# A high part stored 64 bytes further on in a one-core block kernel (convolution, attention, linear attention, mixture of experts)

## The reference, cut to what matters

```python
merged = merged + jax.nn.sigmoid(h @ w_merge_gate[l, n]) * (y_b @ w_branch[l, n])
...
x = x + merged @ w_out[l]
h2 = rms_norm(x, norm_ffn[l])
x = x + hier_moe(h2, ...)
```

## Time and profile before

| What | us |
|---|---|
| median of 3 runs (706.58 to 706.75) | 706.69 |
| the profiled execution's own time | 708.88 |
| its span, first to last instruction | 707.1 |
| PE busy | 584.7 |
| PE weight loads busy (beside PE) | 409.9 |
| DVE busy | 301.2 |
| ACT busy | 191.1 |
| GpSimd busy | 29.7 |

### The profile page before, as it was taken

One profiled execution on the slowest core, in us unless ns is written; L12 is line 12 of the kernel. 1 busy time (PEld: TensorE's weight loads), 2 busy tenths in 40 slices (PEclk: granted clock), 3 DMA queues, 4 the chain that ended last, 5 costly groups with the idle time before them and its releaser, 6 DMA issues.

```text
span 707.1 us, 15475 instructions
## 1 busy us (share of the span) xinstructions
PE 584.7 (83%) x6644; PEld 409.9 (58%) x6644; DVE 301.2 (43%) x627; ACT 191.1 (27%) x335; POOL 29.7 (4%) x58
## 2 busy tenths in 40 slices
PE   7999999999999999996777678666687657778575
PEld 5887899999999885553343334333343324334342
DVE  6476976975475955442222322223222232222312
ACT  5584454564444443111110101001011100111011
POOL 2612000000000020000000000000000000000000
PEclk9999999999999999998787878878779896878987
DMA  9995446446579799999999999999999999999993
GB/s 312 310 362 185 130 145 218 146 149 210 197 273 418 305 388 342 416 426 426 426 428 427 427 425 426 426 425 429 425 426 426 426 428 428 424 426 427 424 415 142
DMA packets 39716, 247.78 MB, mean 350 GB/s; under 512 B 4408, under 2 KB 6592, under 8 KB 25568
## 3 DMA queue, kind: packets, MB, share of 16 engines
q1 hardware_dynamic: 37184, 245.44, 86.0%
q0 software_dynamic: 912, 1.25, 1.0%
q10 hardware_dynamic: 1552, 0.10, 0.2%
HBM read 245.72 MB, written 1.06 MB: 349 GB/s over the span
## 4 chain that ended last, share of the span: by engine, by line
PE 55%; DMA 39%; another core or an unknown queue 2%; DVE 1%; issue 1%; ACT 0%; SPq 0%; DVEq 0%; ACTq 0%
DMA wide<-in_w_expert_up 34%; PE ps L1414 10%; PE ps L1050 7%; PE ps L1052 7%; PE ps L1051 7%; DMA wide<-in_w_expert_down 5%; PE ps L1449 4%; PE ps L1374 3%; PE ps L1023 3%; PE ps L1025 3%; PE ps L1024 3%; PE ps L1461 2%; PE ps L1429 1%; PE ps L1383 1%; DMA x_tok<-in_x 1%
## 5 line engine op out<-in xcount | busy, mean ns | idle before, releaser
L1414 PE MATMUL ps<-wide,xe 128*32 128x256 f32 x2048 | 163.3, 473 | 109.4 <-DMA wide<-in_w_expert_up 108.7
L1414 PEld LDWEIGHTS ps<-wide,xe 128*32 128x32 f32 x2048 | 76.7, 131 | 176.1 <-issue 133.4
L1943 DVE TENSOR_TENSOR xe<-ps,g_ffn 128x256 f32<-128x256 f32 x32 | 13.6, 425 | 256.8 <-PE ps L1383 256.7
L1538 DVE TENSOR_TENSOR ring_lo<-ring,w_hi 128x1024 fp32r<-128x1024 f32 x76 | 91.4, 1222 | 40.2 <-ACT w_hi L745 39.9
L745 ACT ACTIVATE w_hi<-ring 128x1024 fp32r<-128x1024 f32 x76 | 78.9, 1057 | 55.1 <-PE ps L1052 34.9
L1050 PE MATMUL ps<-hT_hi,w_hi 128*128 128x256 f32 x320 | 89.3, 279 | 0.6 <-DVE hT_lo L1554 0.6
L1051 PE MATMUL ps<-hT_lo,w_hi 128*128 128x256 f32 x320 | 88.4, 276 | 0.0
L1052 PE MATMUL ps<-hT_hi,ring_lo 128*128 128x256 f32 x320 | 88.4, 276 | 0.0
L946 ACT ACTIVATE he<-ps 128x128 f32<-128x128 f32 x32 | 8.9, 278 | 207.0 <-PE ps L1429 204.4
L1449 PE MATMUL ps<-wide,he 128*32 128x256 f32 x1024 | 62.5, 382 | 0.9 <-DMA wide<-in_w_expert_down 0.8
L1050 PEld LDWEIGHTS ps<-hT_hi,w_hi 128*128 128x128 f32 x320 | 60.1, 188 | 1.1 <-DVE ring_lo L1538 0.8
(11 more groups left out here) (284 smaller groups left out, 773.7 us busy)
## 6 DMA issues: line engine op xcount, KB each, us to landing
wide<-in_w_expert_gate SPq DMA_DIRECT2D x27, 2048.0 KB, 45.5
wide<-in_w_expert_up SPq DMA_DIRECT2D x27, 2048.0 KB, 48.6
wide<-in_w_expert_down SPq DMA_DIRECT2D x27, 2048.0 KB, 41.1
ring<-in_w_in SPq DMA_DIRECT2D x8, 2048.0 KB, 14.7
ring<-in_w_merge_gate SPq DMA_DIRECT2D x6, 2048.0 KB, 9.8
wide<-in_w_expert_gate SPq DMA_DIRECT2D x10, 1024.0 KB, 13.4
wide<-in_w_expert_up SPq DMA_DIRECT2D x10, 1024.0 KB, 9.3
wide<-in_w_expert_down SPq DMA_DIRECT2D x9, 1024.0 KB, 9.4
```

Source lines behind the costliest of these rows:

```text
L1414: ins = t_.matmul(ps[q * WIN:(q + 1) * WIN, b, 0:QW], xe[b][:, k % 2, k // 2, :], w, start=(k == 0), stop=(k == KD - 1))
L1538: v.tensor_tensor(piece(ring_lo, g, c), piece(ring, g, c), by_row(out_hi[g == 19][c]).bitcast(F32), ALU.subtract).then_inc(wpre_lo, 1)
```

## The change

`out_hi` begins 64 bytes later, now 128 above a multiple of 256 and still from `gv`'s place on. So that its end does not meet `scr`, `scr` and everything that shares its bytes begin 128 bytes later, now 192 above a multiple of 256. No other tile moves, and no instruction, wait, DMA or order of work is added, removed or exchanged.

```diff
@@ -230,13 +230,14 @@
         att_at = here_at[0]
         attm = here("attm", [P, 8, P], F32)
         gv_at = here_at[0]
-        out_hi = [w_hi, [place(f"out_hi{c}", [P, CW], F32R, at=gv_at + 4 * CW * c) for c in range(CHUNKS)]]
+        out_hi = [w_hi, [place(f"out_hi{c}", [P, CW], F32R, at=gv_at + 64 + 4 * CW * c) for c in range(CHUNKS)]]
         gv = here("gv", [P, TT, C], F32)
         gr_at = here_at[0]
         gr = here("gr", [P, TT, C], F32)
         kdn = here("kdn", [P, TT, 256], F32)
         sbd_at = here_at[0]
         sbd = here("sbd", [P, 3, 2, 256], F32)
+        here_at[0] += 2 * 64
         scr_at = here_at[0]
         scr = here("scr", [P, 2, C], F32)
```

## The result

The change makes the kernel slower: 710.19 us median (709.84 to 712.1, five runs) against 706.69 (706.55 to 706.75, five runs). The ratio is 1.0044, with an interval of 1.0026 to 1.0061. The forecast was 706.7 and no difference; the range ended at 707.6.

The account below looks back on a forecast made before the run. PE was taken to bound the kernel until about 275 us, then the expert weights' stream at some 426 GB/s. All terms were zero, so 706.69 + 0 = 706.7 us; the range was 705.9 to 707.6.

Parts of the forecast that it names:

- ACT, DVE and PE on `out_hi`: Operations writing, reading or streaming `out_hi` around the output projection: zero change; PE between 0.45 us less and 0.20 more.
- The row of `ring_lo`: Eight matmuls streaming `ring_lo` at 128 past `merged_hi`: 0.1175 us each, taken as showing that `out_hi` gains nothing at 128.
- `scr` and its sharers: Tiles in `scr`'s bytes, moved to 192: zero, up to 0.46 us more, of which `yc_hi` at the slow pace 0.30.
- The name says only half: Rival at 156 to 168 us: `yc_hi`, not the output projection, moves the time; 0.30 us more, 707.0 us; chance 0.05.
- Two reads of PE meet: Rival on `out_hi` matmuls: load and stream at the same offset modulo 128 delay each other; 0.45 us less, 706.2; chance 0.12.
- The pick of rows: Rival at line 1374, first three experts: picks streaming `xn2_0` each grow 0.5 us; 1.5 us more, 708.2 us; chance 0.05.
- The small terms: GpSimd's `xn2_0` write, `w_z` matmuls, DVE's branch sums and the final store: each taken as zero, with small bounds.
- the estimate: First final store, `fin0`: 134 beats in place of 130 per row, 3% more, landing 0.1 us later.
- Delays of PE reach the end: Before the router's end: a delay of the output projection shifts the DMA gaps and the end, at most one for one.
- The chances: For the kernel's time: 0.87 no difference, 0.06 faster and 0.07 slower by over 0.2%.

Follow-up runs that it names:

- experiment 7: Changed kernel, `yc_hi` back at 64, both `merged` parts at 192: 711.25 us, ratio 1.0046; smaller move, `merged_lo` left at 128, `scr` and `yc_hi` at 64: 708.31 us, 0.9997.

## Why the prediction was wrong

**ACT, DVE and PE on `out_hi`: right.** The tile view of the changed kernel:

```profile
L1264 PE MATMUL ps<-out_hi,merged_hi x32: 274/281/363, 246.5 to 261.8; 128*128 128x256 f32 x32
...
L885 ACT ACTIVATE out_hi<-ring x4: 1042/1042/1044, 239.8 to 242.7; 128x1024 fp32r<-128x1024 f32 x4
L1539 DVE TENSOR_TENSOR ring_lo<-ring,out_hi x4: 1216/1216/1218, 241.1 to 244.5; 128x1024 fp32r<-128x1024 f32 x4
```

ACT went from 1043 to 1042 ns, DVE from 1222 to 1216, the matmuls kept their median of 281. Their pace in the second pass is that of the earlier trace rows, 15 steps in 1.77 us:

```profile
250.68 0.28 PE L1264 MATMUL ps<-out_hi,merged_hi 128*128 128x256 f32 x1
...
252.45 0.28 PE L1267 MATMUL ps<-out_hi,merged_lo 128*128 128x256 f32 x1
```

The chain has this pass and the picks behind it at the same 2.7 us of delay, and with `out_hi` moved alone the kernel is unchanged. The row of `ring_lo` that I chose for this term was the right one for the matmuls that load `merged_hi`. For the other half, which load `merged_lo` at 128, it says nothing: I overlooked that their distance goes from 192 to 0. That they cost nothing is partly luck. Before the change they alternate with matmuls at 0 and 64 and ran at 0.118 already, and experiment 7 shows that the quarters get faster only where all that follow one another lie at 192.

**`scr` and its sharers: the term of the sum that failed is `yc_hi`, taken as zero.** I wrote that "the tiles at 64 and at 128 differ by less than a nanosecond" and that the slow pace would cost at most 64 x 0.0047 = 0.30 us. Both steps fail. The rows that I compared, in the quarters, lie at 64 and at 0 and 192 by turns, and both stretches are slow; that they agree says nothing about a series that lies at 192, the one fast distance, as a whole and is made to leave it. The row that could have said it was in my own hands: the branch's 113.3 against the quarters' 118, which I took as the scale of the effect but not as a sign that the place of `yc_hi` decides. And the bound counted only the matmuls that stream the moved tile. The measured price is 2.99 us, ten times the 0.30, because PE keeps the slow pace through the 608 other matmuls of the unbroken series. The pace per matmul, 0.0047, was right to 0.3 ns.

**The rivals.** *The name says only half* was right about the place (from 156 us, `yc_hi`, not the output projection) and wrong in size, 707.0 for 710. *Two reads of PE meet* had the right kind of mechanism, the relation of streamed and loaded tile, with the wrong rule: not the same offset modulo 128 but one of six distances modulo 256 is the good one, and the new place of `out_hi` does not reach it. *The pick of rows* did not get slower: 1.00 us, as before.

**The small terms: right.** GpSimd's write of `xn2_0`, the matmuls on `w_z`, DVE's sums and the store of the result in the changed kernel, by timeline and tile views:

```profile
258.84 4.03 POOL L705 TENSOR_SCALAR xn<-x_tok,stat 128x1024 f32<-128x1024 f32 x1 [141.66 <-DVE stat L1851]
```

```profile
L1079 PE MATMUL ps<-hT_hi,w_z x16: 379/379/403, 22.7 to 23.8; 128*32 128x256 f32 x16
```

```profile
L1794 DVE TENSOR_TENSOR xn_merged<-xn_merged,scr x8: 691/692/693, 196.3 to 237.6; 128x512 f32<-128x512 f32 x8
```

```profile
DMA to landing us min/median/max: 2.7/3.0/3.4
```

4.03 us against 3.98, 379 ns against 379, 692 ns against 692, and landings of 2.7 to 3.4 us in both the earlier trace rows. The 3% that the Trainium skill's page "DMA: Bandwidth & Descriptors" would add to the first store's beats do not show: that store is the shorter of the two, and in the records it lands 2.69 us after its issue in both kernels, where the estimate asked for 0.1 us more. The measurement decides against the estimate here.

**Delays of PE reach the end: right.** A delay of 2.7 us ahead of the router became 0.44% at the end (3.1 us by the ratio), "at most one for one" within its interval of 1.8 to 4.3 us. The last load in the chain says it more closely, first in the change, then with `out_hi` moved alone:

```profile
667.94 32.12 DMA wide<-in_w_expert_down
```

```profile
665.10 32.09 DMA wide<-in_w_expert_down
```

It begins 2.84 us later in the change, and the first matmul on `out_hi` 3.04 us later (246.47 against 243.43).

**The chances.** 0.07 for slower was too little. The argument that no row shows an effect of the address rested on rows of other pairs of tiles; for a moved operand of a series that was all at its fast distance, the cost was unknown, and the unknown was bounded by the number of its own users.

## What to carry to other kernels

When a tile that PE streams or loads is moved, look at the pair (streamed tile, loaded tile), not at the tile, and ask whether the trace has that distance anywhere; where it does not, count every matmul of the unbroken series behind it, not only those that read the tile. A busy share of 100% hides such a loss: count the instructions in a stretch of fixed length and divide. And where several names share bytes, move them one by one: here the tile that the change was named after did nothing, and an unnamed neighbour did everything.

## What the hardware showed

- **A matmul's pace depends on where its two operands lie.** 256 columns of fp32r past a 128 x 128 load took from 113.3 ns (distance 192) to 120.0 (distance 0) in long series, with the same instructions and PE always 100% busy. Where pairs at 192 alternate with pairs at 0 or 64, as in the quarters, the pace was slow too (0.118 us). The Trainium skill's page "TensorE: Matmul & The Clock Gate", in the section on what each phase is for, says that loading the next weights does not take read bandwidth from the running matmul, since PE has two independent read ports. The runs differ from that as far as the pace goes: with the loads unchanged in number and size, it moves by 6% with the distance of the two reads.
- **At distance 192 there are two paces, 113.3 and 117.8 ns, and an unbroken series keeps its own.** A tile at another distance can push it into the slow one (`yc_hi`, not `ya_hi`); behind one bfloat16 matmul it was slow too; three transposes did not bring the fast pace back; the start behind 1.03 us of idle time had it. Each of the last three was tried at one place only.
- **What stays open.** The records do not show the cause inside PE. In the slow pace each matmul starts some 115 ns after its own load, in the fast one 110, so a fixed rhythm between the two reads is a plausible reading, but it is argued and not shown. Nor is it known what decides the pace of a start: with the feature products' tiles as before, the series at 91 to 150 us started fast in all runs but one, the one at 11 us was slow in two, and which other tiles matter was not tried.
